# Linear attention inside a two-layer backbone: query scaling, key order, state-step slots, output root and branch split placed differently

## The chip, the cores and the metric

The kernel runs on one core of a Trainium2 chip. The metric is the device time of one execution in microseconds (us), lower is better; a statement about "the time" means this. The core has five engines with instruction streams of their own: PE (TensorE, matrix multiply), DVE (VectorE), ACT (ScalarE), POOL (GpSimd) and SP (SyncE, which only issues loads here). They meet at semaphores alone.

## The reference

Two layers over 512 latent tokens and 256 context tokens of width 1024, float32. Each layer is a half-step SwiGLU network, a token mixer, and a second half-step SwiGLU network. The change touches the mixer only. Cut to what matters:

```python
def token_mixer(h, grid, s_f0, s_b0, lp):
    proj = h @ lp['w_in']
    y_gla = gla_branch(proj, s_f0, s_b0, lp) @ lp['w_br_gla']
    y_pool = pool_mix(proj[..., OFF_POOL:OFF_GP], grid, lp['pool_w'], lp['pool_scale']) @ lp['w_br_pool']
    merged = sigmoid(proj[..., OFF_GP:OFF_GG]) * y_pool + sigmoid(proj[..., OFF_GG:IN_COLS]) * y_gla
    return merged @ lp['w_out'], proj

# gated linear attention, chunks of 64 tokens, b = cumulative log gates in the chunk, both directions
q_t = qc * exp(b); k_t = kc * exp(-b); k_end = kc * exp(b_last - b)
att = where(mask, q_t @ k_t^T, 0)
o   = att @ v + q_t @ S_before_the_chunk
S   = S * exp(b_last) + k_end^T @ v          # 12 chunks in a row: the state chain
o   = rmsnorm(o_forward + o_backward) * silu(r)
```

Four heads are worked as two pairs, so each layer has two state chains (pair 0, pair 1) of 11 steps, each step serving both directions. In layer 0 outputs are needed for all 6 blocks of 128 tokens, in layer 1 for the 4 latent blocks only. The context chunks come first in both directions, and they are the last tokens in memory (512 to 767).

## The kernel before

Activations lie with channels on partitions and tokens along the free axis. Each float32 weight tile of 1024 x 128 (a "unit") is split into a rounded high part (`whi`, by ACT, `split_hi`) and a remainder (`wlo`, by DVE, `split_lo`). PE then does three products per chunk of 128 input channels: high x high, high x low, low x high (`unit_products`). Line 1204 has the first two, line 1211 the third. Two slots of `whi` and `wlo` alternate, so a split waits until PE has finished the unit two before.

The plan of a layer is: up/down of the first network, `proj` (keys, gates, queries, values), the "fill" units, `gates` (the two sigmoid gates and the two branch products), `out`, and up/down of the second. The 8 fill units (4 of the pooling input `u`, 4 of `r`, which goes through Silu) are ordinary matrix products with no tie to the attention. The attention's small matmuls are laced between them so that PE has work while DVE and ACT do the attention's elementwise part.

The lacing goes by slots. Fill unit j has slots 12j to 12j+7 behind its eight high chunks and 12j+8, 12j+9, 12j+10 behind pairs of low chunks. `gla_slot(l, kind, pr, i)` gives each piece a due slot: `kend` (the transposes of the keys scaled to the chunk's end), `kv` (a state step's products, line 633), `o` (a block's outputs, line 664; the scores, line 644, come with fixed steps of kv or half a place behind an output) and `var` (the sums for the output's norm). PE issues a piece in the first slot at or after its due number. ACT and DVE use the same numbers only to decide where in their own streams the next unit's split and the draining of a finished fill unit stand (`fill_to`).

The instructions the change and the steps below speak of:

- `key_factors`, `query_factors` (ACT): exponentials into `kt` and `qbd`. `scale_keys`, `scale_queries` (DVE, lines 986 and 991): these times the keys and queries. Scores wait for both.
- `transpose_v` (PE, line 561) turns values into bank 6, and `copy_v` (DVE, line 952) copies them out. The next `transpose_v` waits for that copy, since the bank is the same.
- `kpad`: the transposed end keys, with zeros between chunks. POOL clears it and `qbd` (semaphore `gla_zero`), and `pad_kend` (ACT) fills it.
- `state_step` (DVE, lines 1016 and 1018): four small operations per step. PE may be two steps ahead of it.
- The end: `variances`, then ACT's square root (line 875), DVE's reciprocal (line 1063), then `gates`. `gates_ahead_scalar` and `gates_ahead_vector` hold the pooling products' and the normed outputs' splits (`yphi`, `yplo`, `yghi`, `yglo`).

Of the kernel before, what the change touches and what calls it, by code (L numbers as in the profile page):

```python
# [21 lines left out]
P = 128  # L22
# [128 lines left out]
KV_STEPS = NCH - 1  # L151
FWD = [*range(SEQ // CHUNK, NCH), *range(SEQ // CHUNK)]
# [7 lines left out]
def gla_slot(l, kind, pr=0, i=0):  # L160


    lead, chain, out = (5, 1, 1.5) if l < DEPTH - 1 else (8, 1.6, 2)
    chains = [lead + 4, 0]
    outs = [chains[0] + chain * KV_STEPS + 1, 0]
    chains[1] = outs[0] + 2 * out * blocks(l) + 1
    outs[1] = chains[1] + chain * KV_STEPS + 1
    if kind == "kend":
        return lead + i / 2 if pr == 0 else outs[0] + 2 * out * (1 + i / 2) + out / 2
    if kind == "kv":  # L170
        return chains[pr] + chain * i
# [17 lines left out]
def build(nc, t):  # L189
# [179 lines left out]
    gla_zero = sem("gla_zero")  # L369
# [132 lines left out]
    def fill_ps(j, part):  # L502

        return bank((3, 5)[j % 2]) if part[0] == 0 else bank((4, 2)[j % 2], 0, CTX)
# [63 lines left out]
    def pool_products(pe, l, g):  # L568

        pe.wait_ge(pooled, 4 * l + g + 1)  # L570
# [37 lines left out]
    def kend_bank(pr, d, half):  # L608
        return 1 if pr else (0, 1, 6, 7)[2 * d + half]

    def gla_tensor(pe, l, p0):
# [64 lines left out]
        for d in range(2):  # L676
            yield gla_slot(l, "kend", 0, 2 * d)
            if d == 0:
                pe.wait_ge(pair_free, p0 + 5)
            else:  # L680
                pe.wait_ge(misc_free, MISC * l + 6)
            transpose_kend(0, d, 0)
            yield gla_slot(l, "kend", 0, 2 * d + 1)
            transpose_kend(0, d, 1)
# [1361 lines left out]
```

## Time and profile before

| what | value |
|---|---|
| median of 3 runs | 3166.28 us (3163.28 to 3168.23) |
| the profiled execution, its own time | 3163.74 us |
| its span, first to last instruction | 3161.9 us |
| PE busy | 97% of the span |
| mean granted TensorE clock | 0.986 of 2.4 GHz |
| DVE, ACT, POOL busy | 48%, 26%, 7% |
| DMA, mean | 86 GB/s |

The two mixers' attention parts lie at about 750 to 930 us (layer 0) and 2455 to 2597 us (layer 1) of the span. PEclk in a window is the mean granted clock as a share of the full one. Matmul ends in the trace are modelled and overlap the next start by some tenths, so the rate of PE is read from starts, and its idle time from the bracket behind a row: `[idle before <-releaser]`.

### The profile page before, as it was taken

The numbers are of one execution on the slowest core, as the hardware profiler recorded it, in microseconds if no ns is written. First come the engines' busy times: TensorE is split into PE (matmuls) and PEld (weight loads), VectorE is DVE, ScalarE is ACT, GpSimd is POOL, SyncE is SP. The second block draws the span as 40 slices with busy tenths as digits, with TensorE's granted clock in tenths as the row PEclk, the third lists the DMA queues.
The fourth block names the chain that finished last, engine by engine and source line by source line (L and its number), as shares of the span: only waits on it lengthen the run. The fifth ranks groups of instructions, "written<-read, shape, count | busy, mean of one in ns | idle before, by whom it ended". The sixth has DMA issues, their size and how long they took to land.

```text
span 3161.9 us, 43288 instructions
## 1 busy us (share of the span) xinstructions
PE 3062.2 (97%) x16692; PEld 2604.5 (82%) x16692; DVE 1515.3 (48%) x2649; ACT 809.0 (26%) x1092; POOL 212.5 (7%) x212
## 2 busy tenths in 40 slices
PE   7999999999899999999999999999999889999998
PEld 4888888887778888888888888888888678878886
DVE  2565565557433346565655653222236644443333
ACT  3211211243232222212112311121234333332223
POOL 1000000012500010000000100000010410100001
PEclk9999999999999999999999999999999999999999
DMA  6343434221012214344342332222113113323331
GB/s 205 106 121 107 125 113 127 67 63 41 24 42 62 63 47 134 99 137 129 113 118 85 94 103 60 62 60 65 58 44 81 34 47 90 107 80 93 94 97 62
DMA packets 455603, 273.42 MB, mean 86 GB/s; under 512 B 9754, under 2 KB 453828, under 8 KB 455492
## 3 DMA queue, kind: packets, MB, share of 16 engines
q1 hardware_dynamic: 453348, 267.90, 29.5%
q10 hardware_dynamic: 2144, 4.00, 0.4%
q8 instruction: 75, 1.23, 0.2%
q14 instruction: 36, 0.29, 0.0%
HBM read 269.77 MB, written 2.10 MB: 86 GB/s over the span
## 4 chain that ended last, share of the span: by engine, by line
PE 90%; DVE 6%; ACT 2%; issue 1%; DMA 0%; POOL 0%; ACTq 0%; DVEq 0%; POOLq 0%
PE ps L1204 52%; PE ps L1211 26%; PE ps L1354 2%; PE ps L1275 2%; DVE states L1018 1%; DVE hlo L1699 1%; DVE htmp L1689 1%; PE ps L1359 1%; PE ps L1235 1%; PE ps L1314 1%; PE ps L664 1%; PE ps L644 1%; PE ps L1253 1%; PE ps L633 0%; ACT whi L1448 0%
## 5 line engine op out<-in xcount | busy, mean ns | idle before, releaser
L1204 PE MATMUL ps<-hhi,whi 128*128 128x512 f32 x3136 | 903.5, 355 | 7.2 <-ACT tok L875 7.2
L1204 PE MATMUL ps<-hlo,whi 128*128 128x512 f32 x3136 | 889.1, 351 | 0.0
L1618 DVE TENSOR_TENSOR wlo<-wraw,whi 128x1024 fp32r<-128x1024 f32 x371 | 457.5, 1233 | 677.3 <-ACT whi L1448 673.9
L1448 ACT ACTIVATE whi<-wraw 128x1024 fp32r<-128x1024 f32 x371 | 391.7, 1056 | 1041.9 <-PE ps L1211 1010.2
L1211 PE MATMUL ps<-hhi,wlo 128*128 128x512 f32 x3136 | 632.5, 351 | 0.0
L1204 PEld LDWEIGHTS ps<-hhi,whi 128*128 128x128 f32 x3136 | 504.9, 190 | 91.9 <-issue 11.3
L1204 PEld LDWEIGHTS ps<-hlo,whi 128*128 128x128 f32 x3136 | 503.5, 189 | 85.6 <-issue 0.8
L1211 PEld LDWEIGHTS ps<-hhi,wlo 128*128 128x128 f32 x3136 | 500.8, 188 | 84.4 <-issue 1.0
L1633 DVE SCALAR_TENSOR_TENSOR macc<-modraw,cond,macc 128x256 f32<-128x256 f32 x896 | 365.6, 479 | 0.0
L1204 PE MATMUL ps<-mhi,whi 128*128 128x512 f32 (+1 forms) x1184 | 335.8, 351 | 2.6 <-DVE mlo L1830 1.5
L1204 PE MATMUL ps<-mlo,whi 128*128 128x512 f32 (+1 forms) x1184 | 334.3, 349 | 0.0
L1826 DVE TENSOR_TENSOR mtmp<-ps,stmp 128x512 f32<-128x512 f32 (+1 forms) x154 | 82.7, 573 | 384.6 <-ACT stmp L1569 384.6
L1211 PE MATMUL ps<-mhi,wlo 128*128 128x512 f32 (+1 forms) x1184 | 235.9, 349 | 0.0
L1204 PEld LDWEIGHTS ps<-mhi,whi 128*128 128x128 f32 x1184 | 188.7, 188 | 35.7 <-DVE mlo L1830 2.8
L1204 PEld LDWEIGHTS ps<-mlo,whi 128*128 128x128 f32 x1184 | 188.8, 188 | 32.2
L1211 PEld LDWEIGHTS ps<-mhi,wlo 128*128 128x128 f32 x1184 | 188.8, 188 | 32.2
L1569 ACT ACTIVATE stmp<-ps 128x512 f32<-128x512 f32 (+1 forms) x154 | 70.7, 504 | 557.7 <-PE ps L1211 557.6
L1840 DVE SCALAR_TENSOR_TENSOR x<-ps,gate,x 128x512 f32 (+3 forms) x156 | 89.9, 635 | 176.3 <-PE ps L1211 176.3
L1964 POOL MEMSET ssq<- 128x768 f32 x7 | 5.2, 741 | 2438.6 <-PE ps L1211 2049.6
L1830 DVE TENSOR_TENSOR mlo<-mtmp,mhi 128x768 f32 (+3 forms) x88 | 78.5, 892 | 93.6 <-ACT mhi L1573 93.6
L1573 ACT ACTIVATE mhi<-mtmp 128x768 f32 (+3 forms) x88 | 69.8, 793 | 108.8 <-DVE mtmp L1826 108.8
L1886 POOL TENSOR_TENSOR ssq<-ssq,sq 128x768 f32<-128x768 f32 (+2 forms) x52 | 84.2, 1619 | 163.3 <-ACT sq L1473 79.2
(180 smaller groups left out, 2383.2 us busy)
## 6 DMA issues: line engine op xcount, KB each, us to landing
wraw<-in_ffn_up SPq DMA_DIRECT2D x176, 512.0 KB, 3.9
modraw<-in_w_mod SPq DMA_DIRECT2D x66, 1024.0 KB, 5.2
wraw<-in_ffn_down SPq DMA_DIRECT2D x64, 512.0 KB, 3.7
wraw<-in_w_in SPq DMA_DIRECT2D x64, 512.0 KB, 4.0
wraw<-in_ffn_down SPq DMA_DIRECT2D x32, 384.0 KB, 3.2
wraw<-in_w_out SPq DMA_DIRECT2D x16, 512.0 KB, 3.7
first_mod<-in_w_mod SPq DMA_DIRECT2D x6, 1024.0 KB, 12.2
wraw<-in_w_br_pool SPq DMA_DIRECT2D x16, 256.0 KB, 2.7
```

Of the source, the lines that this page charges most:

```text
L1204: nc.tensor.matmul(o, whi[:, slot, k, :], a[:, k * NT + t0:k * NT + t0 + n], start=(k == 0 and a is hi), stop=False)
L1211: mm = nc.tensor.matmul(o, wlo[:, slot, k, :], hi[:, k * NT + t0:k * NT + t0 + n], start=False, stop=k == kk - 1)
L1275: mm = nc.tensor.matmul(bank(6, 2 * c + h, 1), macc[:, buf, c, h * P:(h + 1) * P], ones[:, 0:1], start=True, stop=True)
L1448: nc.scalar.activation(whi[:, slot2], wraw[:, slot4], ACT.Copy).then_inc(hi_split, 1)
L1569: ins = nc.scalar.activation(stmp[:, h, pt[0]:pt[0] + pt[1]], pair_ps(buf, 0, pt), ACT.Silu)
L1573: nc.scalar.activation(mhi[:, ds((2 * i + h) * NT, c)], mtmp[:, h, 0:c], ACT.Copy).then_inc(mhi_done, 1)
L1618: nc.vector.tensor_tensor(wlo[:, slot2], wraw[:, slot4], whi[:, slot2].bitcast(F32), ALU.subtract).then_inc(lo_split, 1)
L1633: ins = nc.vector.scalar_tensor_tensor(out=macc[:, buf, c, :], in0=modraw[:, buf, k, :], scalar=cond[:, c * DC + k:c * DC + k + 1], in1=ma ...
L1826: ins = nc.vector.tensor_tensor(mtmp[:, h, pt[0]:pt[0] + pt[1]], pair_ps(buf, 1, pt), stmp[:, h, pt[0]:pt[0] + pt[1]], ALU.mult)
L1830: nc.vector.tensor_tensor(mlo[:, ds((2 * i + h) * NT, c)], mtmp[:, h, 0:c], mhi[:, ds((2 * i + h) * NT, c)].bitcast(F32), ALU.subtract).th ...
L1840: ins = nc.vector.scalar_tensor_tensor(out=x[:, ds(n * NT + t0, m)], in0=pair_ps(buf, s, (t0, m)), scalar=gate[:, ds(e * DC + n, 1)], in1= ...
L1886: nc.gpsimd.tensor_tensor(ssq[:, t0:t0 + c], ssq[:, t0:t0 + c], sq[:, j % 2, t0:t0 + c], ALU.add).then_inc(sq_used, 1)
```

## The change

It has five parts.

1. Queries of pair 0 are scaled ahead of the state chain: ACT computes `query_factors(0)` before `key_factors(0)`, POOL clears `qbd` first (the semaphore `gla_zero` is split in `qbd_zero` and `kpad_zero`), and DVE scales the queries before the last value unit's copy and right before the chain. The second direction's key scaling and the two copies of values that are left move one step deeper into the chain.
2. `KEND_ORDER` takes the late tokens' end keys first for both directions, and steps 0 and 1 wait for these two pieces instead of all four.
3. `gla_slot` gives the steps wider places: layer 0 from 1 slot a step to 1.3 (pair 0) and 1.8 (pair 1); layer 1 keeps 1.6 for pair 0 and has 2 instead of 1.6 for pair 1.
4. The square root and the reciprocal stand before the draining of the last fill unit, whose context part goes to bank 7. `gates` starts once six fill units are drained; the first pooling product waits for the seventh and the second for the last.
5. The split of the first branch weights (`w_br_pool`) stands before the normed outputs' splits, on ACT and DVE.

```diff
+KEND_ORDER = ((0, 1), (1, 1), (0, 0), (1, 0))
...
-    lead, chain, out = (5, 1, 1.5) if l < DEPTH - 1 else (8, 1.6, 2)
+    lead, chain, out = (5, (1.3, 1.8), 1.5) if l < DEPTH - 1 else (8, (1.6, 2), 2)
     chains = [lead + 4, 0]
-    outs = [chains[0] + chain * KV_STEPS + 1, 0]
+    outs = [chains[0] + chain[0] * KV_STEPS + 1, 0]
     chains[1] = outs[0] + 2 * out * blocks(l) + 1
-    outs[1] = chains[1] + chain * KV_STEPS + 1
+    outs[1] = chains[1] + chain[1] * KV_STEPS + 1
...
-        return bank((3, 5)[j % 2]) if part[0] == 0 else bank((4, 2)[j % 2], 0, CTX)
+        return bank((3, 5)[j % 2]) if part[0] == 0 else bank(7 if j == FILL - 1 else (4, 2)[j % 2], 0, CTX)
...
-    def pool_products(pe, l, g):
+    def pool_products(pe, l, p0, g):
+        if g == 0:
+            pe.wait_ge(fill_free, (FILL - 1) * (l + 1))
+        if g == 1:
+            pe.wait_ge(pair_free, p0)
...
                 if s == 0:
+                    pe.wait_ge(kpad_ready, 8 * l + 4 * pr + 2)
+                    pe.wait_ge(misc_free, MISC * l + 6 + 2 * pr)
+                    pe.wait_ge(kpad_zero, l + 1)
+                    at_least(pe, o_used, o_before(l, pr))
+                if s == 2:
                     pe.wait_ge(kpad_ready, 8 * l + 4 * pr + 4)
-                    pe.wait_ge(misc_free, MISC * l + 6 + 2 * pr)
-                    pe.wait_ge(gla_zero, l + 1)
-                    at_least(pe, o_used, o_before(l, pr))
                 kv_products(pr, s)
-                if pr == 0 and s in (1, 2):
-                    transpose_v(pe, l, p0, 1 + s)
+                if pr == 0 and s in (2, 3):
+                    transpose_v(pe, l, p0, s)
...
         end_factors(0)
         act.wait_ge(b_ready, 4 * l + 4)
+        act.wait_ge(qbd_zero, l + 1)
+        query_factors(0)
         key_factors(0)
...
-        fill_to(NEVER)
+        fill_to(gla_slot(l, "var", 1, HEADS - 1))
         act.wait_ge(ovar_ready, l + 1)
...
+        fill_to(NEVER)
...
+        split_branch()
         for h in range(HEADS):
...
+                if unit == AHEAD - 1:
+                    scale_queries(dve, l, 0, 0, 0)
+                    scale_queries(dve, l, 0, 0, 1)
...
         scale_keys(0, 0)
-        scale_keys(0, 1)
+        scale_queries(dve, l, 0, 1, 0)
+        scale_queries(dve, l, 0, 1, 1)
         dve.wait_ge(dec_ready, 2 * l + 1)
         for s in range(KV_STEPS):
             fill_to(gla_slot(l, "kv", 0, s))
             state_step(0, s)
-            if s in (1, 2):
-                copy_v(dve, l, 1 + s)
+            if s == 1:
+                scale_keys(0, 1)
             if s in (2, 3):
-                scale_queries(0, s - 2, 0)
-                scale_queries(0, s - 2, 1)
+                copy_v(dve, l, s)
...
                             if gates_first:
-                                pe.wait_ge(pair_free, p0)
+                                pe.wait_ge(fill_free, (FILL - 1) * l + FILL - 2)
                                 pe.wait_ge(o_used, o_before(l, 1) + blocks(l))
                                 pe.wait_ge(ostd_ready, l + 1)
```

How the order moves at three places. DVE's stream in layer 0, from the value copy ahead of pair 0's chain to its fifth step. Before (`L1016`, `L1018` are state steps, `L991` queries, `L986` keys, `L952` values, `L1618` a weight split):

```order
L1618 TENSOR_TENSOR wlo<-wraw,whi 128x1024 [waits hi_split]
L986 TENSOR_TENSOR kt<-kq,kt 128x768 [waits ekt_ready] x2
L1016 COPY states<-ps 64x128 [waits kv_ready,dec_ready]
...
L1018 SCALAR_TENSOR_TENSOR states<-states,dec,ps 64x128 [waits kv_used,kv_ready]
...
L952 COPY vt<-ps 128x6x128 [waits misc_ready]
...
L952 COPY vt<-ps 128x6x128 [waits misc_ready]
L991 TENSOR_TENSOR qbd<-kq,qbd 64x768 [waits eq_ready] x2
L1018 SCALAR_TENSOR_TENSOR states<-states,dec,ps 64x128 [waits kv_used,kv_ready]
L1018 SCALAR_TENSOR_TENSOR states<-states,dec,ps 64x128 x3
L991 TENSOR_TENSOR qbd<-kq,qbd 64x768 [waits eq_ready] x2
L1618 TENSOR_TENSOR wlo<-wraw,whi 128x1024 [waits hi_split]
```

And the same stretch of the changed kernel (there `L1031`, `L1033` are state steps, `L990` queries, `L1008` keys, `L967` values, `L1635` a weight split):

```order
L1635 TENSOR_TENSOR wlo<-wraw,whi 128x1024 [waits hi_split]
L1008 TENSOR_TENSOR kt<-kq,kt 128x768 [waits ekt_ready]
L990 TENSOR_TENSOR qbd<-kq,qbd 64x768 [waits eq_ready] x2
L1031 COPY states<-ps 64x128 [waits kv_ready,dec_ready]
...
L1008 TENSOR_TENSOR kt<-kq,kt 128x768 [waits ekt_ready]
L1033 SCALAR_TENSOR_TENSOR states<-states,dec,ps 64x128 [waits kv_used,kv_ready]
L1033 SCALAR_TENSOR_TENSOR states<-states,dec,ps 64x128 x3
L967 COPY vt<-ps 128x6x128 [waits misc_ready]
L1033 SCALAR_TENSOR_TENSOR states<-states,dec,ps 64x128 [waits kv_used,kv_ready]
L1033 SCALAR_TENSOR_TENSOR states<-states,dec,ps 64x128 x3
L967 COPY vt<-ps 128x6x128 [waits misc_ready]
L1635 TENSOR_TENSOR wlo<-wraw,whi 128x1024 [waits hi_split]
```

The four query products have left the chain (two of them stand 10 rows further up, before the values' units are copied), one key product has come in behind step 1, and each value copy stands one step later.

PE's stream in layer 0 at steps 1 to 3 of the same chain. Before (`L633` is a step's products, `L561` the value transposes):

```order
L633 MATMUL ps<-vt,kpad 128x256 x2
L561 MATMUL ps<-ident,vf 128x128 [waits pair_free,misc_free]
L561 MATMUL ps<-ident,vf 128x128 x5
...
L1204 MATMUL ps<-hlo,whi 128x256
L633 MATMUL ps<-vt,kpad 128x256 [waits kv_used]
L633 MATMUL ps<-vt,kpad 128x256
L561 MATMUL ps<-ident,vf 128x128 [waits pair_free,misc_free]
L561 MATMUL ps<-ident,vf 128x128 x5
L633 MATMUL ps<-vt,kpad 128x256 [waits kv_used]
```

Of the changed kernel, steps 1, 2 and 3 (`L642` the products, `L566` the transposes):

```order
L642 MATMUL ps<-vt,kpad 128x256 x2
L642 MATMUL ps<-vt,kpad 128x256 [waits kv_used,kpad_ready]
L642 MATMUL ps<-vt,kpad 128x256
L566 MATMUL ps<-ident,vf 128x128 [waits pair_free,misc_free]
L566 MATMUL ps<-ident,vf 128x128 x5
...
L1221 MATMUL ps<-hlo,whi 128x256
L642 MATMUL ps<-vt,kpad 128x256 [waits kv_used]
L642 MATMUL ps<-vt,kpad 128x256
L566 MATMUL ps<-ident,vf 128x128 [waits pair_free,misc_free]
L566 MATMUL ps<-ident,vf 128x128 x5
```

Steps 1 and 2 (due 10.3 and 11.6) share slot 12, because 11 is no slot; step 3 comes in slot 13, one high chunk later, and the second group of transposes right behind it.

ACT's stream at the end of layer 0's fill units. Before:

```order
L1448 ACTIVATE whi<-wraw 128x1024 [waits w_used,w_loaded2]
L801 ACTIVATE bsum<-ps 128x256 [waits w_used]
L801 ACTIVATE bsum<-ps 128x512
L875 ACT_TABLE_LOAD
L875 ACTIVATE tok<-ps,eps 128x24 [waits ovar_ready]
L884 ACTIVATE yphi<-ps,vecs 128x768 [waits misc_ready] x4
L888 ACTIVATE yghi<-kq 128x768 [waits oy_ready] x4
L1448 ACTIVATE whi<-wraw 128x1024 [waits w_used,w_loaded3]
```

Of the changed kernel:

```order
L885 ACT_TABLE_LOAD
L885 ACTIVATE tok<-ps,eps 128x24 [waits ovar_ready]
L1465 ACTIVATE whi<-wraw 128x1024 [waits w_used,w_loaded2]
L810 ACT_TABLE_LOAD
L810 ACTIVATE bsum<-ps 128x256 [waits w_used]
L810 ACTIVATE bsum<-ps 128x512
L895 ACTIVATE yphi<-ps,vecs 128x768 [waits misc_ready] x4
L1465 ACTIVATE whi<-wraw 128x1024 [waits w_used,w_loaded3]
L900 ACTIVATE yghi<-kq 128x768 [waits oy_ready] x4
```

The root is ahead of the last drain, a second table load stands between them, and the branch weights' split is ahead of `yghi`.

## Rows read from the trace of the kernel before

**Rows 1.** The page: the span, and busy time by engine.

```profile
span 3161.9 us, 43288 instructions
PE 3062.2 (97%) x16692; PEld 2604.5 (82%) x16692; DVE 1515.3 (48%) x2649; ACT 809.0 (26%) x1092; POOL 212.5 (7%) x212
```

**Rows 2.** Waits of PE, 730 to 960 us: total us, times, longest.

```profile
PE ps L644 <- DVE qbd L991: 10.7, 2, 7.0
PE ps L1204 <- ACT tok L875: 3.8, 1, 3.8
PE ps L633 <- DVE states L1016: 2.8, 1, 2.8
PE ps L633 <- DVE states L1018: 1.9, 3, 0.8
PE ps L1204 <- ACT whi L1448: 1.6, 1, 1.6
```

**Rows 3.** Waits of PE, 2430 to 2650 us, same columns.

```profile
PE ps L644 <- DVE qbd L991: 5.7, 2, 3.9
PE ps L633 <- DVE states L1018: 4.1, 4, 1.4
PE ps L1204 <- ACT tok L875: 3.5, 1, 3.5
PE ps L664 <- DVE states L1018: 3.4, 2, 2.3
PE ps L561 <- DVE vt L952: 2.0, 1, 2.0
PE ps L1204 <- ACT whi L1448: 1.9, 2, 1.6
PE ps L633 <- ACT kpad L831: 1.3, 1, 1.3
```

**Rows 4.** Windows: length; busy of PE, PEld, DVE, ACT, POOL; PEclk; DMA share; GB/s.

```profile
771.00:776.00 5.00, 4.38 (x12) 3.65 (x13) 3.17 (x6) 0.00 (x0) 3.91 (x6) 0.54 0.43 101
...
899.00:902.00 3.00, 3.00 (x9) 2.62 (x10) 0.08 (x1) 0.00 (x0) 0.31 (x1) 0.51 0.66 174
```

**Rows 5.** Timeline of PE, layer 0, pair 0: start us, us, instruction.

```profile
734.34 2.99 PE L1211 MATMUL ps<-hhi,wlo 128*128 128x512 f32 x16
...
771.62 2.05 PE L644 MATMUL ps<-qbd,kt 128*128 128x256 f32 x4 [7.05 <-DVE qbd L991]
...
787.05 0.71 PE L664 MATMUL ps<-att,vt 128*128 128x128 f32 x4 [0.49 <-DVE states L1018]
```

**Rows 6.** Timeline of DVE, the same stretch.

```profile
747.26 1.95 DVE L914 TENSOR_SCALAR vf<-ps 128x512 f32<-128x512 f32 x4 [5.87 <-PE ps L561]
...
758.59 1.43 DVE L1018 SCALAR_TENSOR_TENSOR states<-states,dec,ps 64x128 f32<-64x128 f32 x4 [0.31 <-PE ps L633]
760.04 0.96 DVE L952 COPY vt<-ps 128x768 f32<-128x768 f32 x1
...
768.14 3.34 DVE L991 TENSOR_TENSOR qbd<-kq,qbd 64x768 f32<-64x768 f32 x2
```

**Rows 7.** Timeline of ACT, the same stretch.

```profile
740.41 1.57 ACT L816 ACTIVATE kt<-bsum 128x768 f32<-128x768 f32 x2
...
755.82 3.42 ACT L822 ACTIVATE qbd<-bsum 64x768 f32<-64x768 f32 x4
```

**Rows 8.** Timeline of DVE, layer 0, pair 1.

```profile
819.09 1.19 DVE L1016 COPY states<-ps 64x128 f32<-64x128 f32 x4
...
821.84 1.19 DVE L986 TENSOR_TENSOR kt<-kq,kt 128x768 f32<-128x768 f32 x1
...
835.76 1.91 DVE L991 TENSOR_TENSOR qbd<-kq,qbd 64x768 f32<-64x768 f32 x1
```

**Rows 9.** Timeline of ACT, layer 0, end of the fill units.

```profile
897.17 1.28 ACT L875 ACT_TABLE_LOAD   x1
898.46 0.28 ACT L875 ACTIVATE tok<-ps,eps 128x24 f32<-128x24 f32 x1
```

More of the change, by code:

```diff
@@ L170, in gla_slot @@
     if kind == "kv":
-        return chains[pr] + chain * i
+        return chains[pr] + chain[pr] * i
     if kind == "o":
@@ L515, in is_split_ahead, with is_branch_ahead @@
         return (follows_norm(ph) or ph["kind"] == "gates") and isinstance(i, int) and i == h == 0 and s == 1
+    def is_branch_ahead(ph, i, h, s):
+        return ph["kind"] == "gates" and isinstance(i, int) and i == h == 0 and s == 2
     def peeled(ph, a):
@@ L674, in variances @@
                 mm.then_inc(ovar_ready, 1)
-        for d in range(2):
-            yield gla_slot(l, "kend", 0, 2 * d)
-            if d == 0:
+        for i in range(4):
+            yield gla_slot(l, "kend", 0, i)
+            if i == 0:
                 pe.wait_ge(pair_free, p0 + 5)
-            else:
+            if i == 2:
                 pe.wait_ge(misc_free, MISC * l + 6)
-            transpose_kend(0, d, 0)
-            yield gla_slot(l, "kend", 0, 2 * d + 1)
-            transpose_kend(0, d, 1)
+            transpose_kend(0, i)
         for pr in range(2):
@@ L734, in onorm_tensor, with gates_steps @@
             mm.then_inc(obc_ready, 1)
-    def gates_steps(pe, l, buf, unit, slot):
+    def gates_steps(pe, l, p0, buf, unit, slot):
         if unit == 0 and slot in (1, 4, 7, 10):
-            pool_products(pe, l, (1, 4, 7, 10).index(slot))
+            pool_products(pe, l, p0, (1, 4, 7, 10).index(slot))
         if unit == 1 and slot == 1:
@@ L841, in gla_scalar @@
         split_hi(unit, unit % 4, unit % 2)
-        act.wait_ge(gla_zero, l + 1)
-        for d in range(2):
-            for half in range(2):
-                fill_to(gla_slot(l, "kend", 0, 2 * d + half))
-                pad_kend(0, d, half)
-        query_factors(0)
+        act.wait_ge(kpad_zero, l + 1)
+        for i in range(4):
+            fill_to(gla_slot(l, "kend", 0, i))
+            pad_kend(0, i)
         for pr in range(2):
@@ L1560, in body @@
                             if kind == "gates" and h == 0 and isinstance(i, int) and i == 0:
-                                gates_ahead_scalar(act, l)
+                                gates_ahead_scalar(act, l, lambda: split_hi(unit + 2, (u0 + 2) % 4, u0 % 2))
                             for s in range(1, 3):
                                 if not (isinstance(i, int) and ph is plan[-1] and 2 * i + h == ph["pairs"] - 1 and s == 2) \
-                                        and not is_split_ahead(ph, i, h, s):
+                                        and not is_split_ahead(ph, i, h, s) and not is_branch_ahead(ph, i, h, s):
                                     split_hi(unit + s, (u0 + 2 * h + s) % 4, (u0 + s) % 2)
@@ L1816, in body @@
                                 mod_accumulate(job, (j0 + h) % 2, range(DC // 2))
-                            if not (isinstance(i, int) and ph is plan[-1] and 2 * i + h == ph["pairs"] - 1):
+                            if not (isinstance(i, int) and ph is plan[-1] and 2 * i + h == ph["pairs"] - 1) \
+                                    and not is_branch_ahead(ph, i, h, 2):
                                 split_lo(unit + 2, (u0 + 2 * h + 2) % 4, u0 % 2)
```

63 lines of the change are left out of this document (34 added, 29 removed).

## The prediction

> **What bounds the kernel now.** I read the page first: PE is busy 97% of a span of 3161.9 us [rows 1]. The loads, at 86 GB/s, never appear among the mixers' waits. So time can come only from PE's idle stretches, from what its clock does after them, or from PE work, and this change neither removes nor adds a matmul. Next I read the waits of PE alone, in the two mixers. In layer 0 its idle time adds up to 22.6 us, of which 10.7 is for scaled queries, 3.8 for the output root, 2.8 for a first state copy and 1.6 for the branch weights' split [rows 2]. In layer 1 it is 23.3 us: queries 5.7, state steps 4.1 and 3.4, root 3.5, a value copy 2.0, the branch splits 1.9, the padded keys 1.3 [rows 3]. Nearly every microsecond cut there comes off the end, since PE runs full before and after.
>
> The third view is the clock. After the 7.05 us wait PE ran 771 to 776 at a granted clock of 0.54, which is mostly the 1.2 GHz level in place of 2.4, and after the root's wait 899 to 902 at 0.51 [rows 4, 5]. At half rate a stretch costs half its length: 2.3 us and 1.5 us on top of the waits. So a long wait removed is worth more than itself.
>
> **Rates.** Sixteen low matmuls (four slots) take 2.99 us, the last one's tail of some 0.15 included [rows 5], so a slot is 0.71 us of PE in layer 0. With one token part it is about two thirds of that, 0.47, in layer 1. A step's four products or a pair of scores take some 0.86 between the rest, six transposes 0.6. On DVE a state step is 1.43 and a value copy 0.96 [rows 6].
>
> **Part 1 and 2, first chain of layer 0.** Moving two query products ahead of 747.26 costs nothing: DVE idled 5.87 us there [rows 6]. ACT computes their exponentials (3.42 for four) where it did the keys' (1.57) at 740.4 [rows 7]; first direction ready at about 742, second at 744, keys 745.4, all before use. If this cover were gone, 1.9 us (0.95 each, below) would push the last value copy. The trace has no 64x768 product with POOL quiet; the last two took 1.67 each, POOL busy [rows 6], which is the upper bound; the lower one is the value copy's 0.96, of the same length, and I take that, since POOL only clears memory there. The other two stand before step 0 and end at about 755.7, when DVE would wait for step 0's products anyway.
>
> What is late next: DVE began step 1 at 758.59 with its products in slot 10 [rows 6]. Now steps 1 and 2 stand together in slot 12, two slots (1.4) later, less the 0.36 that PE waited for keys before. So DVE: step 1 759.6 to 761.0; key product to 762.3 (1.19 with POOL busy [rows 8]; 0.9 if not); step 2 to 763.8; value copy to 764.7. PE reaches the second value transposes behind step 3 at 762.4 and must wait for that copy: a new wait of about 2.3 us. Before, the first value copy stood behind step 1, at 760.04 [rows 6], and no wait of layer 0 names it. The scores no longer wait. Behind it DVE has a split and steps at 1.43 against PE's 1.6 to 2.3 per step, so it keeps up; outputs start at 783.5 in slot 25. Before they started at 787.05 in slot 21 [rows 5], four slots (2.8) less work done. Gain: 787.05 + 2.83 - 783.5 = **6.4**, with about 1.8 of low clock after the new wait charged. Without that low clock it would be 8.2; with the wait at 4 us, 4.
>
> Here the Trainium skill has a rule against the change (SBUF — State Buffer, Who interferes with whom): a DVE instruction with two SBUF inputs and a GpSimd instruction that reads SBUF exclude each other for a whole instruction. POOL's pooling starts some 2 us earlier now, under the key product. By the rule that product could be held for a full POOL operation, and the new wait would be about 1 us longer; the row's 1.19 for a product beside a busy POOL is what the sum uses.
>
> **First chain of layer 1.** Slots are unchanged. The waits were 1.3 (keys), 2.0 (value copy), 3.9 (queries), 2.3 (outputs) [rows 3]: 9.5. The first and third go. The second stays and grows to 2.5, since the key product (1.2) stands ahead of the copy where only a split and a step did; the fourth stays at 2.3, as DVE still has a split and four steps in a row ahead of them. So 1.3 + 3.9 - 0.5 = 4.7 of waits go, and the low clock behind the query wait, as in layer 0, some 2.0: **6.7**.
>
> **Part 3, second chains.** Layer 0: DVE worked without a break from 819.09 to the last query product's end at 837.67, 18.6 us, keys at 1.19 and queries up to 1.91 [rows 8], and PE waited 2.8, 1.9 in three and 3.7 for it, 8.4 [rows 2]. The 2.84 came of a split that ACT made late, behind its exponentials; due numbers of 37 against an output's 39.3 now put it ahead. From step 0's products ready to the scores PE now has 12 slots and eight steps, 8.5 + 6.9, less the 1.1 for step 0 itself: 14.3. DVE has its 18.6, plus 1.3 because the next split (due 49) now falls before step 4 instead of behind the queries, plus 0.9 of idling before step 1, two slots on: 20.8. PE waits the difference, 6.5 against 8.4, most of it (3.6) at the scores, and the 1.5 of low clock behind the 2.8 goes: **3.4**. If the split were hidden too, 4.7; if its place cost double, 2.1. Layer 1: DVE sets the end of the queries, PE has two slots more (0.93) to fill the wait, and the last wait of 1.1 before the outputs goes: **2.0**.
>
> **Part 4, the root.** The sums' last matmuls stand at slot 87 of 96; the table load (1.28) runs ahead of its wait and the root takes 0.28 [rows 9], done long before the unit ends, in layer 1 by 0.4 us. The waits of 3.8 and 3.5 go, with 1.4 of low clock each: **10.1**. ACT pays a second table load, 1.28, before the last Silu. Split, load and Silu take 1.05 + 1.28 + 0.9 = 3.2 us behind the unit's end in layer 0. The second pooling product needs it after five slots (3.5) and the first pooling product. In layer 1 it is 2.9 against 2.3 and a pooling product of some 0.9, so priced at 0, at worst 0.6. The Trainium skill (ScalarE: Activation LUTs, What ACT_TABLE_LOAD costs) adds a drain of about 1.38 us to each switch. By it the layer 1 drain would come at 4.3 and cost 1.1 us, sum 30.0. In the trace the root starts 1.29 us after its load began, so the sum leaves that drain out.
>
> **Part 5.** PE waited 1.6 in each layer for the split behind the last `yghi` [rows 2, 3]. With it gone, the next is the second branch weights' split, behind the sigmoid's table load: about 0.15 us late in layer 0 and 0.6 in layer 1. Gain 1.5 + 1.0 = **2.5**. DVE's split ahead of the norm's products delays them by 0.3 to 0.8, under PE's gate products.
>
> **Sum.** 6.4 + 6.7 + 3.4 + 2.0 + 10.1 + 2.5 = 31.1. The profiled execution took 3163.7, so 3132.6; the median of runs lies 2.5 above it, so **3135**.
>
> **Rivals.** (a) DVE is the chains' real limit and the waits move more than they shrink. For: the value copies and the key product replace the queries in the chain, and POOL is busy beside them. Against: four query products of 6 us did leave it. If both new value waits are 4 us and the second layer 0 chain gains nothing, 4 + 5.2 + 0 + 2.0 + 12.6 = 24 less at most; with low clock after each, 17: 3149. (b) The first chains gain nothing at all, because a transposed value wait follows both copies: parts 3 to 5 alone, 18, 3148, or only 4 and 5, 12.6, 3153. (c) More: the 2.3 and 2.5 waits do not lower the clock, and POOL disturbs less: 37 to 41, 3125 to 3129. (d) Slower: waits of 1.3 to 2.5 us now come every few steps, and the clock stays at 1.2 GHz between them instead of rising again. Each us of matmul work at that level adds one; the chains hold some 16 + 20 us per layer. It needs over 31 us of extra work at the low level to end slower, some 40 of 72: 3172. Against: the mean granted clock of the whole run is 0.986 with 46 us of such waits in it, so it rose again each time.
>
> **How the numbers follow.** A measurement of this kernel tells about 0.2%, 6.3 us, from no change. The forecast holds 0.64 (own range 3129 to 3143), (a) 0.13, (b) 0.09, (c) 0.08, (d) 0.03; 0.03 is left for a cost not listed. Range 3126 to 3151. Faster takes all but (d) and that rest.
>
> **What would show it.** In the waits of PE: no row for queries in the first chains, one of 2 to 2.5 us for the value copy in each layer, queries still 3 to 4 in layer 0's second chain, no root row, a branch row under 0.7. Idle sums of 22.6 and 23.3 fall to about 11 and 13. Wrong it would be if the transposes wait over 4 us, if the clock row of the chains falls under 0.85, or if PE waits at the second pooling product.

## The result and the profile after

The changed kernel takes 3128.44 us, median of 4 runs (3127.09 to 3131.01); before it was 3166.38 in the same session (3163.28 to 3168.23). The ratio is 0.9882, 95% interval 0.9869 to 0.9896: 37.9 us less. The forecast was 3135, range 3126 to 3151, faster at 0.94. The direction and the range held; the gain was 6.8 us larger than the sum of 31.1. The median lies 0.6 below the 3129 to 3143 that the forecast called its own and inside the 3125 to 3129 of rival (c), which had a chance of 0.08.

The page of the changed kernel, its profiled execution of 3129.19 us:

```profile
span 3127.4 us, 43300 instructions
PE 3052.9 (98%) x16692; PEld 2597.6 (83%) x16692; DVE 1511.2 (48%) x2649; ACT 810.9 (26%) x1094; POOL 213.0 (7%) x212
```

PE has the same 16692 matmuls as in [rows 1], and ACT two instructions more, the second table load of each layer. The waits of PE in layer 0's mixer, columns as in [rows 2]:

```profile
PE ps L653 <- DVE qbd L990: 2.5, 1, 2.5
PE ps L642 <- DVE states L1033: 2.4, 3, 1.7
PE ps L566 <- DVE vt L967: 1.9, 1, 1.9
PE ps L633 <- DVE bsum L984: 0.5, 1, 0.5
PE ps L633 <- ACT kpad L841: 0.5, 1, 0.5
PE ps L1221 <- ACT whi L1465: 0.3, 1, 0.3
```

And in layer 1's, where [rows 3] stood:

```profile
PE ps L642 <- DVE states L1033: 3.2, 4, 1.0
PE ps L653 <- DVE qbd L990: 2.8, 1, 2.8
PE ps L673 <- DVE states L1033: 2.3, 1, 2.3
PE ps L566 <- DVE vt L967: 2.1, 1, 2.1
PE ps L1221 <- ACT whi L1465: 1.2, 1, 1.2
PE ps L633 <- ACT kpad L841: 1.2, 2, 0.7
PE ps L741 <- DVE yplo L1087: 0.2, 1, 0.2
```

The idle sums are 8.1 and 13.0, from 22.6 and 23.3: 24.8 us less. No row names the root's `tok`, and one query row per layer is left where there were two waits. The rest is clock. I went through both mixers in windows of half a microsecond and marked where the granted clock was half. Before, that was 20.5 us in layer 0 and 13.7 in layer 1; after, 3.4 and 6.8. Half of the 24.0 that went is 12.0, the time it had cost. 24.8 + 12.0 = 36.8 accounts for the two mixers. The two profiled executions lie only 34.6 apart, since that of the changed kernel reached layer 0's mixer 2.65 us late: it had run the first 100 us at a lower clock (0 to 50 us at 0.92 against 0.97, 50 to 100 at 0.91 against 0.93), before any instruction that the change touches. Matmul by matmul, from PE's starts, the gain is 22.4 in layer 0's mixer and 14.7 in layer 1's, 37.1 in all. Windows of the changed kernel (columns as in [rows 4]): behind the value copy's wait, behind the query wait, in the last fill unit, and behind the value copy's wait of layer 1:

```profile
766.00:770.00 4.00, 3.06 (x19) 2.77 (x20) 3.86 (x7) 0.00 (x0) 1.68 (x5) 1.00 0.00 0
831.00:835.00 4.00, 2.90 (x15) 2.59 (x16) 2.34 (x5) 0.00 (x0) 3.48 (x8) 1.00 0.00 0
874.80:878.20 3.40, 3.40 (x11) 2.87 (x12) 0.30 (x1) 0.28 (x1) 0.00 (x0) 0.51 0.13 38
2448.50:2451.50 3.00, 3.00 (x11) 2.62 (x11) 2.17 (x5) 0.00 (x0) 1.34 (x2) 0.50 0.00 0
```

Three waits, of 1.86, 2.50 and 2.81 us, had no low clock behind them; two, of 2.12 and 2.28 (ahead of layer 1's outputs, low at 2469), had; and the clock fell once with PE at work throughout (3.40 of 3.40 us). That was the surprise, and the experiments turned on it.

DVE in layer 0's first chain, changed kernel, where [rows 6] had the queries:

```profile
762.03 1.43 DVE L1033 SCALAR_TENSOR_TENSOR states<-states,dec,ps 64x128 f32<-64x128 f32 x4 [1.72 <-PE ps L642]
763.49 0.96 DVE L1008 TENSOR_TENSOR kt<-kq,kt 128x768 f32<-128x768 f32 x1
764.47 1.43 DVE L1033 SCALAR_TENSOR_TENSOR states<-states,dec,ps 64x128 f32<-64x128 f32 x4
765.93 0.96 DVE L967 COPY vt<-ps 128x768 f32<-128x768 f32 x1
```

PE waited 1.86 us for that copy and got on at 766.94. The predicted order is there: a step, the key product, a step, the copy.

### The profile page after: what moved, and what is told of

Read it like the earlier page. It is cut to its first block, busy times and chain, and to the rows that moved or that the text cites. A ratio compares the mean times of both kernels' runs of the same rounds, so it can differ in the third digit from the quotient of the medians.

```text
span 3127.4 us, 43300 instructions
## 1 busy us (share of the span) xinstructions
PE 3052.9 (98%) x16692; PEld 2597.6 (83%) x16692; DVE 1511.2 (48%) x2649; ACT 810.9 (26%) x1094; POOL 213.0 (7%) x212
## 4 chain that ended last, share of the span: by engine, by line
PE 91%; DVE 5%; ACT 2%; issue 1%; DMA 0%; POOL 0%; ACTq 0%; DVEq 0%; POOLq 0%
PE ps L1221 53%; PE ps L1228 27%; PE ps L1371 2%; PE ps L1292 2%; PE ps L1252 1%; PE ps L1376 1%; PE ps L1331 1%; DVE hlo L1716 1%; DVE states L1033 1%; DVE htmp L1706 1%; PE ps L673 1%; PE ps L1270 1%; PE ps L642 1%; PE ps L653 1%; PE ps L557 0%
## 5 line engine op out<-in xcount | busy, mean ns | idle before, releaser
L1635 DVE TENSOR_TENSOR wlo<-wraw,whi 128x1024 fp32r<-128x1024 f32 x371 | 456.8, 1232 | 654.7 <-ACT whi L1465 651.0
```

The lines of the kernel that those rows point to most:

```text
L1635: nc.vector.tensor_tensor(wlo[:, slot2], wraw[:, slot4], whi[:, slot2].bitcast(F32), ALU.subtract).then_inc(lo_split, 1)
```

## The experiments

Each is an edit of the changed kernel, but for e4, which is that kernel again. In the table, "waits" is PE's idle time in the two mixers by the rows of waits, and "low" the time at half clock there by half-microsecond windows, layer 0 / layer 1, both of the profiled execution, whose own time stands beside the median.

| kernel | median | profiled | waits | low |
|---|---|---|---|---|
| before | 3166.38 | 3163.74 | 22.6 / 23.3 | 20.5 / 13.7 |
| changed | 3128.44 | 3129.19 | 8.1 / 13.0 | 3.4 / 6.8 |
| e4 changed, again | 3128.20 | 3127.82 | 8.0 / 13.0 | 3.4 / 6.8 |
| e1 old slots | 3136.50 | 3136.20 | 12.9 / 13.9 | 6.8 / 0 |
| e2 queries back | 3145.18 | 3145.90 | 12.9 / 19.2 | 10.2 / 13.7 |
| e3 root back | 3142.90 | 3141.08 | 11.7 / 16.5 | 17.1 / 6.8 |
| e5 key order back | 3131.71 | 3128.58 | 8.3 / 14.1 | 6.8 / 3.4 |
| e6 branch back | 3131.17 | 3133.03 | 9.4 / 13.6 | 10.2 / 6.8 |
| e7 copy first | 3126.73 | 3126.30 | 7.2 / 12.6 | 3.4 / 3.4 |
| e8 scores late | 3123.82 | 3123.50 | 5.6 / 11.4 | 0 / 6.8 |
| e10 e7 and e8 | 3121.81 | 3121.41 | 5.1 / 11.3 | 0 / 0 |
| e11 first chain too | 3121.07 | 3121.16 | 4.7 / 10.0 | 0 / 3.4 |
| e12 delay | 3133.74 | 3134.72 | 8.1 / 13.0 | 6.8 / 6.8 |
| e13 root alone | 3154.23 | 3154.23 | 18.8 / 19.4 | 17.1 / 6.8 |

**The account closes.** Profiled time less both waits less half of both low columns is 3103.0 for the changed kernel (3129.19 - 21.1 - 5.1), 3100.7 for the one before, and between 3100.9 and 3106.0 for all the others (e12 less the 3.9 of its added work). The waits and the low clock of the mixers explain times from 3121 to 3164 us with a remainder that spreads over 5.3 us. So the account can't decide about edits that differ by less.

**The parts add up in waits and not in time.** Undone one at a time, in the order slots, queries, root, key order, branch, the parts bring back 5.7, 11.0, 7.1, 1.3 and 1.9 us of waits. Less the 1.7 that two of the edits share (see e2), that is 25.3, against the 24.8 that went with all five. In medians they cost 8.1, 16.7, 14.5, 3.3 and 2.7, which is 45.3 against 37.9. Low clock doesn't add up so: in the mixers it makes 15.4 of the one sum and 12.0 of the other, and some of what is left lies outside them (see e1).

### Control (e4)

> The changed kernel once more, nothing edited, as a control for the others. All theories: 3128 to 3131 us, waits of PE 8 to 10 us in layer 0's mixer and 12 to 14 in layer 1's. The theory that the low-clock stretch in layer 0's last fill unit (3.4 us of PE, no wait ahead of it) is caused by what stands just ahead of it, two groups of twelve one-column sums, says that it comes back at the same matmuls and that layer 0's chains again have none behind the waits of 1.9 and 2.5 us. Its rival, that the clock falls at moments of its own, says that it is found elsewhere, or nowhere, in this profile.

3128.20 us (3127.82 to 3128.86), ratio 0.9882 (0.9867 to 0.9897). Waits and low stretches came back at the same matmuls, the one in the last fill unit too. That fitted a cause in the stream just ahead, the two groups of twelve one-column sums of squares (1.39 us each). Experiment e7 speaks against it: it has both groups at the same places of the last fill unit, and nothing falls. The same holds of e1 and e8. Windows of e7, then of e4:

```profile
874.00:878.00 4.00, 4.00 (x24) 3.50 (x25) 0.30 (x1) 0.28 (x1) 0.00 (x0) 1.00 0.15 45
```

```profile
874.00:877.00 3.00, 3.00 (x11) 2.51 (x11) 0.24 (x1) 0.00 (x0) 0.00 (x0) 0.50 0.02 7
```

So the sums alone don't lower the clock; the theory fell.

### The slots back (e1)

```diff
-    lead, chain, out = (5, (1.3, 1.8), 1.5) if l < DEPTH - 1 else (8, (1.6, 2), 2)
+    lead, chain, out = (5, (1, 1), 1.5) if l < DEPTH - 1 else (8, (1.6, 1.6), 2)
```

> Part 3 undone: state steps at 1 slot each in layer 0 and 1.6 in both chains of layer 1, the rest as changed. My theory: the wider places give PE fill work while DVE works, so without them PE waits for state steps and queries: layer 0's chains wait 4 to 8 us more in sum and part of that at a low clock; layer 1's second chain 1 to 2 more. Time 3135 to 3141, 6 to 12 above the changed kernel. Rival: with the queries out of the first chain DVE keeps up anyway, and the fill work only stands elsewhere: 0 to 2 above.

3136.50 us, ratio 0.9907 (0.9892 to 0.9923): 8.1 above the changed kernel. In layer 0 the state copy's wait is back and the query wait longer:

```profile
PE ps L653 <- DVE qbd L990: 3.7, 1, 3.7
PE ps L642 <- DVE states L1033: 3.0, 4, 1.1
PE ps L642 <- DVE states L1031: 2.9, 1, 2.9
PE ps L566 <- DVE vt L967: 1.2, 1, 1.2
```

The waits explain 5.7, of which 1.7 is given back by 3.4 us less at half clock. That leaves some 3 to 4 us of the 8.1 that stand in neither column. They are low clock outside the mixers: over the rest of the trace e1 has 61.4 us at half clock and the changed kernel 54.3, which is worth 3.5. One of e1's stretches, between the mixers, has no counterpart in the changed kernel:

```profile
2363.00:2366.40 3.40, 3.40 (x10) 2.60 (x9) 3.33 (x7) 1.79 (x3) 0.00 (x0) 0.50 0.00 0
```

So, as far as these rows tell, that rest is no part of what the slots are worth. For all fourteen profiles together, this term doesn't narrow the spread of the account. The first chain's value wait is shorter with the old slots (1.2 against 1.9). The rival (0 to 2) is out.

### The queries back (e2)

```diff
-                    pe.wait_ge(kpad_ready, 8 * l + 4 * pr + 2)
+                    pe.wait_ge(kpad_ready, 8 * l + 4 * pr + 4)
...
-                if pr == 0 and s in (2, 3):
-                    transpose_v(pe, l, p0, s)
+                if pr == 0 and s in (1, 2):
+                    transpose_v(pe, l, p0, 1 + s)
...
-        query_factors(0)
         key_factors(0)
...
             pad_kend(0, i)
+        query_factors(0)
...
-                if unit == AHEAD - 1:
-                    scale_queries(dve, l, 0, 0, 0)
-                    scale_queries(dve, l, 0, 0, 1)
...
-        scale_queries(dve, l, 0, 1, 0)
-        scale_queries(dve, l, 0, 1, 1)
+        scale_keys(0, 1)
...
-            if s == 1:
-                scale_keys(0, 1)
+            if s in (1, 2):
+                copy_v(dve, l, 1 + s)
             if s in (2, 3):
-                copy_v(dve, l, s)
+                scale_queries(dve, l, 0, s - 2, 0)
+                scale_queries(dve, l, 0, s - 2, 1)
```

> Part 1 undone, with step 0 waiting for all four padded pieces: pair 0's query products, key products and value copies stand where they stood before the change. The wider places, the new key order, the root and the branch split stay. My theory: the wait for queries comes back in both first chains, about 4 to 6 us in layer 0 (7.0 before, less the slots that the wider places add) and 3.9 in layer 1, with low clock behind each, against value waits of 1.9 and 2.1 that go: 3135 to 3141, 7 to 12 above the changed kernel. Rival: the wider places alone had covered the queries, 0 to 3 above.

3145.18 us, ratio 0.9935 (0.9922 to 0.9949): 16.7 above, more than expected. The query waits, layer 0's, are

```profile
PE ps L653 <- DVE qbd L987: 7.9, 2, 5.4
```

and 7.8 in two in layer 1. Of the first chain's wait 5.4 and 5.0 are back; 11.0 of waits in all, and 13.7 us more at half clock, which cost 6.8. Of the 11.0, 1.7 are waits for padded keys (0.4 and 1.3), since this edit also lets step 0 wait for all four pieces again; they belong to part 2. The wider places cover 1.6 of the old 7.0 in layer 0 and no more. In layer 1 the wait is 5.0 where 3.9 was expected, and why is open. By its waits, 9.3 without those for the keys, part 1 was the largest single part.

### The root back (e3), and the root alone (e13)

```diff
-        fill_to(gla_slot(l, "var", 1, HEADS - 1))
+        fill_to(NEVER)
         act.wait_ge(ovar_ready, l + 1)
...
                              bias=eps[:, 0:1], scale=1.0 / DV).then_inc(ostd_ready, 1)
-        fill_to(NEVER)
```

(and the same for DVE's reciprocal)

> Part 4's root undone: square root and reciprocal stand again behind the draining of the last fill unit, bank 7 for its context part and the pooling products' waits stay. My theory: the root waits of 3.8 and 3.5 us come back with 1.4 of low clock behind each, 10.1 in all by the prediction's sum: 3137 to 3140. Rival: since one table switch a layer less stands on ACT, and the last unit of layer 0 lost 1.5 to low clock only in the changed kernel, 6 to 8: 3134 to 3137.

3142.90 us, ratio 0.9929 (0.9915 to 0.9942): 14.5 above the changed kernel, where 10.1 was the sum. The root's waits are back to a tenth (3.8 and 3.5), PE in layer 0:

```profile
PE ps L1219 <- ACT tok L885: 3.8, 1, 3.8
```

The 7.3 us of them are half of it; the other 6.9 is low clock in layer 0, 13.7 us more of it. But not all of that stands behind the root: 6.8 us does, 3.4 follows the value copy's wait and 3.4 the query wait. In layer 1, 3.4 us stands behind the root, but the mixer has no more of it in all than before the edit. Here is PE behind the value copy's wait in e3, 120 us before the root,

```profile
765.83 0.87 PE L566 MATMUL ps<-ident,vf 128*128 128x128 f32 x6 [1.86 <-DVE vt L966]
766.46 0.59 PE L1219 MATMUL ps<-hhi,whi 128*128 128x512 f32 x2
766.89 0.65 PE L1219 MATMUL ps<-hlo,whi 128*128 128x512 f32 x2
767.34 0.84 PE L1219 MATMUL ps<-hhi,whi 128*128 128x512 f32 x2
767.98 0.84 PE L1219 MATMUL ps<-hlo,whi 128*128 128x512 f32 x2
```

and in the changed kernel run again (e4):

```profile
765.74 0.88 PE L566 MATMUL ps<-ident,vf 128*128 128x128 f32 x6 [1.86 <-DVE vt L967]
766.37 0.59 PE L1221 MATMUL ps<-hhi,whi 128*128 128x512 f32 x2
766.80 0.52 PE L1221 MATMUL ps<-hlo,whi 128*128 128x512 f32 x2
767.16 0.51 PE L1221 MATMUL ps<-hhi,whi 128*128 128x512 f32 x2
767.50 0.52 PE L1221 MATMUL ps<-hlo,whi 128*128 128x512 f32 x2
```

From 744 us on both had run the same instructions with starts 0.09 us apart, and both waited 1.86 us. One fell to 1.2 GHz and the other did not. With the same wait, e6 fell too; the changed kernel, e5, e8 and e12 did not. At the 2.5 us query wait of the second chain e2, e3, e5, e6, e7 and e12 fell, the changed kernel and e4 did not. The Trainium skill (TensorE: Matmul & The Clock Gate, Part 1: The HAM clock gate) says that what watches PE's activity runs free and does not restart with a kernel; this pair of rows fits that. That the changed kernel's stretches came back at the same matmuls in e4 doesn't follow from it.

If some of the 14.5 are such stretches that fell elsewhere, the root alone must be worth less:

> Of the five parts only the root stays (with bank 7 and the waits of the pooling products); queries, key order, slots and branch split are as before. Theory: the root's 7.3 us of waits and the low clock behind each go whatever the chains do: 10 to 11 below the kernel before, 3155 to 3156. Rival: undoing the root alone cost 14.6, and if that were its true worth, this kernel would be 14 to 15 below, 3151 to 3152; then the parts would help each other nowhere. If it is 10 to 11, the 4 more were low-clock stretches that fell elsewhere in that kernel.

3154.23 us, ratio 0.9964 (0.9950 to 0.9978) against 3165.85 for the kernel before on that chip: 11.6 less. That is nearer to the 10.1 than to 14 to 15, but the interval, 7.0 to 15.8, holds both, so it's the rows that decide. It undoes the other four parts as e1, e2, e5 and e6 do, and its waits are those of [rows 2, 3] to 0.4, without the root. In the kernel before, one stretch of 3.4 us at half clock stood behind each root wait; both are gone here. That is 7.3 + 3.4 = 10.7. In e3 the stretch behind layer 0's root was 6.8 long, which makes 12.4, and one stretch more than in the changed kernel fell elsewhere, 1.7: 14.1 of the 14.5. So 10 to 12 us is the root's own worth by the rows, and the rest of e3 is where stretches fell.

### The delay (e12)

```diff
-        for b in range(NBLK):
-            mm = nc.tensor.transpose(bank(6, b * P, P), vf[:, g % 2, b * P:(b + 1) * P], ident[:])
+        for k in range(4 if g == 1 else 1):
+            for b in range(NBLK):
+                mm = nc.tensor.transpose(bank(6, b * P, P), vf[:, g % 2, b * P:(b + 1) * P], ident[:])
```

> The changed kernel with 18 extra transposes of 128x128 in each layer ahead of the first fill unit (the six of the value group repeated three times more, the same result), where DVE idles: all that follows comes 1.7 us later in each layer and nothing else moves. If the instruction stream decided where the clock falls, it would fall in layer 0 at the same matmuls as in the changed kernel and the time would be 3131 to 3132. My theory, that a wait of some 2 us lowers the clock or not by where it happens to lie in time: the waits stay (8 and 13 us in sum) but other ones are followed by a low clock, each stretch for 1.7 us, and the time can be anything from 3128 to 3137.

3133.74 us (3130.93 to 3136.74), ratio 0.9898 (0.9883 to 0.9913): 5.3 above. The value unit ahead of the fill units takes 11.10 us from start to start in place of 9.13, in each layer, so 3.9 is the added work, and one more stretch in layer 0 is 1.7. The waits are the same to a tenth, 8.1 and 13.0. The clock fell behind the query wait of layer 0, where the changed kernel's had not (first row), and behind that of layer 1, at 2512, instead of behind the value copy:

```profile
833.00:836.00 3.00, 3.00 (x8) 2.45 (x9) 1.20 (x4) 0.00 (x0) 2.49 (x8) 0.50 0.00 0
...
2512.50:2515.50 3.00, 3.00 (x8) 2.35 (x8) 1.29 (x5) 0.00 (x0) 0.00 (x0) 0.50 0.29 87
```

Its four runs spread over 5.8 us, those of e4 over 1.0. The last-unit stretch came back here, so e12 doesn't show that moving everything moves every stretch; it shows that the waits don't fix them. It is by these rows and not by the time: with the 3.9 of added work the unmoved clock would give 3132.4, which the four runs hold too.

### Key order back (e5), branch split back (e6)

e5 restores `KEND_ORDER = ((0, 0), (0, 1), (1, 0), (1, 1))` and lets step 0 wait for `kpad_ready` at `8 * l + 4 * pr + 4`. e6 passes `lambda: None` for the split ahead of the normed outputs and lets `is_branch_ahead` be false.

> Part 2 undone: the end keys in their old order, and step 0 waits for all four padded pieces. My theory: PE waits again for the padded keys ahead of step 0, 0.4 us in layer 0 and 1.3 in layer 1, and everything behind moves by that much: 3130 to 3132, 1.3 to 1.7 above the changed kernel, if the clock falls where it does there. Rival: the wait of 1.3 in layer 1 shortens the value copy's wait behind it (2.1 to 0.8), since DVE goes on working, and nothing is lost: 0 to 0.5.

> Part 5 undone: the first branch weights are split behind the normed outputs again. My theory: the waits of PE for these splits go back from 0.3 to 1.6 us in layer 0 and from 1.2 to 1.9 in layer 1, 2.0 in all: 3130 to 3131. Rival: the root stands earlier now, so ACT is at the splits earlier and the late split is covered anyway: 0 to 0.5 above the changed kernel.

e5: 3131.71 us (3128.58 to 3132.03), ratio 0.9894 (0.9878 to 0.9911). The waits for padded keys are back as before, 0.4 and 1.3, and the value copy's in layer 1 is only 0.2 shorter. Of the 3.3 above the changed kernel 1.3 are waits; the interval holds 1.3 and 3.3 alike, so its size is not settled. e6: 3131.17 us, ratio 0.9891 (0.9875 to 0.9908), 2.7 above; the splits' waits are 1.6 and 1.9 again from 0.3 and 1.2, the expected 2.0. Both rivals, that something covers the edit, are out by these rows.

### Two small edits towards a better kernel (e7, e8, e10, e11)

e7:

```diff
-            if s == 1:
-                scale_keys(0, 1)
             if s in (2, 3):
                 copy_v(dve, l, s)
+            if s == 2:
+                scale_keys(0, 1)
```

e8:

```diff
-                if s in ((4, 5), (7, 9))[pr]:
+                if s in ((4, 5), (8, 10))[pr]:
```

> The second direction's key product of pair 0 (0.96 us on DVE) moves from behind step 1 to behind the value copy of step 2, so that the copy for which PE waits 1.86 us in layer 0 and 2.12 in layer 1 comes that much sooner. My theory: both waits shrink to about 0.9 and 1.15, the scores still do not wait: 1.9 less, 3126 to 3127, and 3 to 5 less if with the shorter wait the clock fall in layer 1 goes as well. Rival: the key product comes too late for the first scores and PE waits there instead: 3128 to 3130.

> Pair 1's scores stand behind steps 8 and 10 instead of 7 and 9, one fill slot or two later, where PE waits 2.5 us (layer 0) and 2.8 (layer 1) for the last query product. My theory: that wait shrinks by PE's work in between, 0.86 for the step and its slots 1.3 to 1.4 (layer 0), 0.9 (layer 1): 2.3 and 1.7 less, 4 in all: 3124 to 3125. Rival: what DVE still has to do is the same, so the next step waits for the state step instead and only a part is won: 1 to 2 less, with the outputs' wait of 2.3 in layer 1 longer.

e7: 3126.73 us, ratio 0.9882 (0.9866 to 0.9899), not told from the changed kernel. The value copy's waits shrink to 1.0 and 1.2, as expected, but the scores now wait 0.2 and 0.6 for the other copy: DVE works without a break there, and PE meets it at the next place. e8: 3123.82 us, ratio 0.9870 (0.9854 to 0.9887), 4.6 less. The query wait of layer 0 is gone and that of layer 1 down to 0.6, for 0.7 more at the state steps. Layer 1:

```profile
PE ps L642 <- DVE states L1033: 3.9, 6, 1.0
PE ps L673 <- DVE states L1033: 2.2, 1, 2.2
PE ps L566 <- DVE vt L967: 2.1, 1, 2.1
...
PE ps L653 <- DVE qbd L990: 0.6, 1, 0.6
```

e10 is both edits. e11, on top of e8:

```diff
-                if s == 2:
+                if s == 1:
                     pe.wait_ge(kpad_ready, 8 * l + 4 * pr + 4)
                 kv_products(pr, s)
-                if pr == 0 and s in (2, 3):
-                    transpose_v(pe, l, p0, s)
-                if s in ((4, 5), (8, 10))[pr]:
+                if pr == 0 and s in (1, 3):
+                    transpose_v(pe, l, p0, 2 + s // 2)
+                if s in ((5, 6), (8, 10))[pr]:
```

with DVE's copies behind steps 1 and 3, the key product behind step 2 and the masks at steps 6 and 7.

> Both small edits together: the key product behind the value copy of step 2, and pair 1's scores behind steps 8 and 10. My theory: the waits saved add up, 0.7 to 0.9 in layer 0's first chain, 0.4 in layer 1's, 2.4 and 1.7 in the second chains: 5.2 to 5.4 below the changed kernel plus or minus one low-clock stretch of 1.7: 3121 to 3125, and within 1.7 of the kernel with the scores alone. Rival: the two gains collide, DVE being the limit of both chains: no better than the scores alone, 3124.

> Besides the scores of pair 1 behind steps 8 and 10: in pair 0's chain the third value group is transposed and copied behind step 1 instead of 2, the key product follows step 2, and the scores and their masks stand one step later (behind 5 and 6). My theory: PE has no wait over 0.3 us left in layer 0's first chain, and none for the value copy in layer 1's, against 1.9 and 2.1: 4 us below the kernel with pair 1's scores moved alone, 3119 to 3122. Rival: DVE works without a break from step 1 to the fourth value copy, so PE waits as long one place further, at a state step or the outputs: 0 to 1.5 below, 3122 to 3125.

e10: 3121.81 us (3119.93 to 3122.58), ratio 0.9860 (0.9845 to 0.9875); e11: 3121.07 us (3120.90 to 3123.98), ratio 0.9861 (0.9846 to 0.9877). Both are some 7 us under the changed kernel and 44 under the one before, and the same within the measurement. In e10 the waits are 4.7 less than in the changed kernel, where 5.2 was expected, and only 0.6 less than in e8; its other gain over e8 is low clock. In e11 the value copy's row is gone, but layer 0's state steps wait 3.2 in place of e8's 2.2, 0.95 of it in the first chain, where at most 0.3 was expected. So about half of the wait of 1.86 moved on to the next step, as the rival had it, and half went. In e10 no window of either mixer shows a low clock.

## Why the prediction was right, and where its sum was off

These are the terms of the prediction's sum, each with the time that went there by PE's starts in both traces:

| term | predicted | measured |
|---|---|---|
| layer 0, first chain | 6.4 | 8.7 |
| layer 0, second chain | 3.4 | 8.6 |
| layer 0, root | 5.2 | 5.3, less 1.5 of low clock in the last fill unit |
| layer 0, branch | 1.5 | 1.3 |
| layer 1: first chain, second chain, root, branch | 6.7, 2.0, 4.9, 1.0 | 7.3, 1.3, 5.1, 1.0 |

**Right.** The mechanism held: each wait that was to go went, the new one came, and time followed waits and clock. Layer 1 came out at 14.7 for 14.6, but by luck: its first chain gave 0.6 more and its second 0.7 less, and its clock fell behind just the waits that the sum had left it at. The new value-copy wait is there, 1.86 and 2.1 for 2.3 and 2.5. The outputs' wait of layer 1 stayed at 2.3, the root's rows went, the branch's next wait is 0.3 and 1.2 for 0.15 and 0.6, and no row of waits names a pooling product. Moving two query products ahead of the chain cost nothing, at the lower of the two prices (two in 1.92 and two in 1.91 us). The second two, changed kernel:

```profile
756.51 1.91 DVE L990 TENSOR_TENSOR qbd<-kq,qbd 64x768 f32<-64x768 f32 x2
```

Of the signs named, four missed: layer 0's idle sum is 8.1 for 11, its query wait 2.5 for 3 to 4, its value copy's wait 1.9 for 2 to 2.5, and layer 1's branch row 1.2 for under 0.7. The second table load did cost ACT 1.28 and PE nothing; ACT, at the end of layer 0's fill units:

```profile
882.18 1.06 ACT L1465 ACTIVATE whi<-wraw 128x1024 fp32r<-128x1024 f32 x1 [7.06 <-PE ps L1228]
883.26 1.28 ACT L810 ACT_TABLE_LOAD   x1
884.55 0.87 ACT L810 ACTIVATE bsum<-ps 128x256 f32<-128x256 f32 x2
```

Silu starts 1.29 us after the load began, so the drain that the Trainium skill (ScalarE: Activation LUTs, What ACT_TABLE_LOAD costs) adds isn't seen, and the sum of 30.0 by it was the worse one. In layer 1 the Silu starts 1.29 us behind the start of its load too.

**Wrong in size, the clock.** "About 1.8 of low clock after the new wait charged": none came in this kernel's profiles. "The 1.5 of low clock behind the 2.8 goes": all 4.5 us of cost in that chain went, also behind the query wait that stayed. These two sentences hold 1.8 + 3.0 = 4.8 of the 7.5 by which layer 0's two chains were short; the stretch in the last fill unit, foreseen by nobody, takes 1.5 back. They took each wait of about 2 us or more to lower the clock surely. e3 and e4 show that it may or may not, each stretch for 1.7 us, so this term was a draw and not a sum. Rival (c), 37 to 41, had named the outcome, though only half of its reason held: layer 0's new wait didn't lower the clock and layer 1's did. With the clock as the sum had it, the time would have come 3 to 5 us nearer to 3135, so that the gain is 38 and not 33 to 35 is luck. It isn't settled why the draw repeats so well from run to run of one kernel (e4 spread 1.0 us over four).

**Wrong in size, DVE's work.** "DVE has its 18.6, plus 1.3 ... plus 0.9" took the four query products and the two key products ahead of them as before. In the changed kernel, DVE in layer 0's second chain, they read

```profile
815.70 1.72 DVE L1008 TENSOR_TENSOR kt<-kq,kt 128x768 f32<-128x768 f32 x1
...
818.90 1.49 DVE L1008 TENSOR_TENSOR kt<-kq,kt 128x768 f32<-128x768 f32 x1
...
821.87 1.60 DVE L990 TENSOR_TENSOR qbd<-kq,qbd 64x768 f32<-64x768 f32 x1
...
825.99 0.95 DVE L990 TENSOR_TENSOR qbd<-kq,qbd 64x768 f32<-64x768 f32 x1
...
828.44 0.97 DVE L990 TENSOR_TENSOR qbd<-kq,qbd 64x768 f32<-64x768 f32 x1
...
830.77 1.18 DVE L990 TENSOR_TENSOR qbd<-kq,qbd 64x768 f32<-64x768 f32 x1
```

The queries take 4.7 us in all for 6.0 before (1.15, 1.56, 1.41 and the 1.91 of [rows 8]), the keys 3.2 for 2.6 (1.19 and 1.43). From step 0's copy to the last query DVE needed 19.9 in place of the 20.8 reckoned. PE waited 4.9 there and not 6.5: 1.6 of gain, 0.9 of it from DVE. The other 0.7 is that PE's own work in between took some 15.0 us where 14.3 had been reckoned. The idle time of DVE before step 1, put at 0.9, was 0.98.

**Wrong, the step on POOL.** "POOL's pooling starts some 2 us earlier now" was false. POOL waits for the last value transposes, which the change moved back:

```profile
768.04 0.24 POOL L1942 COPY racc<-u 128x64 f32<-128x64 f32 x1 [23.04 <-PE ps L566]
```

The key product at 763.49 had POOL quiet and took 0.96 for the 1.19 taken, half of the value wait's error. What the Trainium skill says (SBUF — State Buffer, Who interferes with whom), weighed there against the change, had nothing to act on in that chain. In the second chain the key products of 1.72 and 1.49 above ran with pooling beside them, against this 0.96.

## What to carry to other kernels

Take waits off the one engine that bounds the kernel by moving work that is ready early into a place where its engine idles, and follow that engine to where it is next met: e7 and e11 moved about half of a wait to the next place, e8 removed most of one, because it let the late engine finish under work already there. Add up waits and half-rate time separately. Most waits came within half a microsecond of their forecast here, two were 1.1 and 1.6 off. The clock behind waits of about 2 us is a draw of 1.7 us each, so give it a range, and judge an edit worth 1 to 3 us by its wait rows too, and not by its time alone.

## What the runs showed of the hardware that was not expected

The low-clock stretches of all fourteen profiles were 3.4 or 6.8 us long in the mixers, with a cost of 1.7 or 3.4. A wait of 1.86 us at the same place lowered the clock in two of seven profiles, and one of 2.5 us in six of eight; layer 1's of 2.81 us did so in five of eight. So within this range the length of the wait alone doesn't decide. The clock also fell in the last fill unit, with no wait ahead, in the changed kernel, e3 to e6 and e12, and not in e1, e2, e7, e8, e10 and e11. A DVE product of 64x768 took 0.96 us with POOL idle (756.51). With POOL's pooling beside it, it took from 0.95 (825.99) to 1.91 us, and one of 128x768 up to 1.72, for 0.96.
